# Latent attention's chunk mask: from a bf16 product per score tile to four contraction rows

## What is computed

```python
def attend_mla(q, q_pos, k, v, k_pos):
    s = jnp.einsum('bqhd,bkhd->bhqk', q, k).astype(jnp.float32) * (MLA_QK ** -0.5)
    mask = (k_pos[None, :] // CHUNK) <= (q_pos[:, None] // CHUNK)      # CHUNK = 64
    s = jnp.where(mask[None, None], s, -jnp.inf)
    w = jax.nn.softmax(s, axis=-1).astype(v.dtype)
    return jnp.einsum('bhqk,bkhd->bqhd', w, v)
```

## Time and profile before

| | |
|---|---|
| median of three runs | 1484.28 us |
| span of the profiled execution | 1481.9 us |
| TensorE (PE) busy | 1391.2 us, 94% |
| PE weight load busy | 1121.9 us, 76% |
| VectorE (DVE) busy | 798.2 us, 54% |
| ScalarE (ACT) busy | 637.7 us, 43% |
| latent attention, layer 0 | 206 to 275 us |
| latent attention, layer 1 | 939 to 1008 us |

### The profile page before, as it was taken

One profiled execution on the slowest core, in us unless ns is written; L12 is line 12 of the kernel. 1 busy time (PEld: TensorE's weight loads), 2 busy tenths in 40 slices (PEclk: granted clock), 3 DMA queues, 4 the chain that ended last, 5 costly groups with the idle time before them and its releaser, 6 DMA issues.

```text
span 1481.9 us, 20955 instructions
## 1 busy us (share of the span) xinstructions
PE 1391.2 (94%) x8418; PEld 1121.9 (76%) x8418; DVE 798.2 (54%) x1159; ACT 637.7 (43%) x931; POOL 90.8 (6%) x84
## 2 busy tenths in 40 slices
PE   5998999999999989999889999999999999899996
PEld 5994665799999856777579856558999987567763
DVE  4427534633435347887662383455343444578876
ACT  5327644522324244656343385444222232355651
POOL 0310000000000011100203000000000000110002
PEclk9999998999999989999989999989999999999998
DMA  8233300033225357998812102000233163599965
GB/s 270 72 101 104 114 1 0 1 114 113 64 68 213 158 226 268 412 414 319 269 57 74 60 21 94 1 1 29 86 113 106 39 238 128 216 347 412 415 230 195
DMA packets 95415, 228.45 MB, mean 154 GB/s; under 512 B 14378, under 2 KB 64580, under 8 KB 82372
## 3 DMA queue, kind: packets, MB, share of 16 engines
q1 hardware_dynamic: 83252, 179.58, 33.6%
q0 software_dynamic: 7424, 30.94, 5.9%
q10 hardware_dynamic: 4656, 16.78, 2.8%
HBM read 198.73 MB, written 33.79 MB: 157 GB/s over the span
## 4 chain that ended last, share of the span: by engine, by line
PE 84%; DVE 6%; ACT 5%; DMA 3%; issue 2%; SPq 0%; ACTq 0%; DVEq 0%; POOLq 0%
PE ps L843 10%; PE ps L845 10%; PE ps L844 10%; PE ps L1316 8%; PE ps L1292 4%; PE ps L1294 4%; PE ps L1293 4%; PE ps L1138 3%; PE ps L869 3%; PE ps L872 2%; PE ps L1099 2%; PE ps L875 2%; DMA rows_back<-xrow_d,row_of 2%; PE ps L1279 2%; PE ps L1195 2%; PE ps L1193 2%
## 5 line engine op out<-in xcount | busy, mean ns | idle before, releaser
L1854 DVE TENSOR_TENSOR work<-work,ps 128x544 f32<-128x544 f32 x48 | 34.6, 721 | 208.9 <-ACT work L1673 208.9
L1673 ACT ACTIVATE work<-ps 128x544 f32<-128x544 f32 x48 | 30.0, 626 | 244.9 <-PE ps L845 244.9
L844 PE MATMUL ps<-xn_r,ksv_r 128*128 128x272 f32 x384 | 110.7, 288 | 0.0
L844 PE MATMUL ps<-xn_r,work_r 128*128 128x272 f32 x384 | 110.7, 288 | 0.0
L761 POOL DMA_INDIRECT rows_back<-xrow_d,row_of x32 | 38.2, 1195 | 1120.9 <-DVE row_of L2229 904.4
L1294 PE MATMUL ps<-ew_r,rows_tok_r 128*128 128x512 f32 x256 | 100.0, 391 | 0.0
L1854 DVE TENSOR_TENSOR ew_r<-ew,gu_hi_a_r 128x2048 fp32r<-128x2048 f32 x32 | 73.1, 2290 | 15.4 <-ACT gu_hi_a_r L1696 15.4
L844 PEld LDWEIGHTS ps<-xn_r,ksv_r 128*128 128x128 f32 x384 | 72.2, 188 | 0.0
L844 PEld LDWEIGHTS ps<-xn_r,work_r 128*128 128x128 f32 x384 | 72.2, 188 | 0.0
L1696 ACT ACTIVATE gu_hi_a_r<-ew 128x2048 fp32r<-128x2048 f32 x32 | 60.7, 1908 | 5.6 <-ACT yo_b L1741 5.6
L1316 PE MATMUL ps<-ew,acts 128*128 128x512 f32 x128 | 58.4, 599 | 1.4 <-DVE acts L2346 1.4
(11 more groups left out here) (401 smaller groups left out, 3930.8 us busy)
## 6 DMA issues: line engine op xcount, KB each, us to landing
wr<-in_w_in SPq DMA_DIRECT2D x68, 512.0 KB, 4.7
ew<-in_w_exp_gate SPq DMA_DIRECT2D x32, 1024.0 KB, 7.2
ew<-in_w_exp_up SPq DMA_DIRECT2D x32, 1024.0 KB, 10.9
ew<-in_w_exp_down SPq DMA_DIRECT2D x32, 1024.0 KB
wr<-in_w_out SPq DMA_DIRECT2D x16, 512.0 KB, 4.3
rows_d<-yo_a ACTq DMA_DIRECT2D x14, 512.0 KB
rows_d<-yo_b ACTq DMA_DIRECT2D x14, 512.0 KB
rows_d<-in_zeros POOLq DMA_DIRECT2D x10, 512.0 KB, 9.7
```

What stands on the lines that cost most here:

```text
L844: mm(out_[h], w_hi, x_lo[:, c], start=False, stop=False, skip_group_check=True)
L1854: return v_.tensor_tensor(o_, a, b, op)
```

## The change

The mask becomes part of the product. Keys and queries get four more contraction rows, 96 to 99, one for each query tile x: the keys' row x is -1e30 for the last 64 keys of tile x and zero elsewhere, the queries' row x is 1 for the first 64 queries of tile x and zero elsewhere. The rows are computed on the host (`chunk_rows`) as two new constants, and SyncE loads them in each layer into `kT` and `qT`, 4 partitions of 6400 and of 4352 numbers, before the loop of the gate weights. TensorE waits for both before its first score product. The sample's units keep 96 rows. The semaphore `reload_` becomes `masks_then_x`, which counts 32 for the two loads and 48 after the residual rows. Three of the 12 fills go.

```diff
--- before.py
+++ after.py
@@ -40,6 +40,7 @@
 C_POOL, C_Q, C_KV, C_KR = 0, 256, 512, 640
 C_QS, C_KS, C_VS, C_GATE = 672, 928, 1184, 1440
 HEADS, NOPE, VD, QK = 8, 64, 64, 96
+MR = SEQ // P
 SBH = 4
 HR = ROPE // 2
 NE, NG, EPG, DE = 16, 4, 4, 256
@@ -70,7 +71,7 @@
 K_ID, K_NTRI, K_STRI, K_COS, K_SIN, K_INVC, K_JL, K_VALID, K_STEP, K_TILE, K_E128, K_IOTA, K_TOK = (
     sum(n for _, n in CONST_COLS[:i]) for i in range(len(CONST_COLS)))
 NCONST = sum(n for _, n in CONST_COLS)
-DVE_FILLS = 12
+DVE_FILLS = 9
 TAIL = NE - 2
 JOINT_BANKS = [0, 2, 4, 0, 2]
 END_BANKS = [0, 2, 4, 6, 0]
@@ -115,8 +116,6 @@
         tok_w = sb("tok_w", [P, 2, NTILE, 4], FP16)
         ident_h = sb("ident_h", [P, P], FP16)
         sums_r = sb("sums_r", [P, 2, P], F32R)
-        negrow = sb("negrow", [1, 64], BF16)
-        halfrow = sb("halfrow", [1, P], BF16)
         ident_b = sb("ident_b", [P, P], BF16)
         late_b = sb("late_b", [P, P], BF16)
         rt = sb("rt", [P, 1252 + 80])
@@ -338,7 +337,7 @@
         xn_rdy = sem("xn_rdy", DC + 1)
         ones_in = (xn_rdy[0], DC + 1, DC)
         spill = sem("spill", 16 + 16 * NTILE)
-        reload_ = sem("reload", 16)
+        masks_then_x = sem("masks_then_x", 32 + 16)
         tk_mm = sem("tk_mm", 20)
         tk_ev = sem("tk_ev", 20)
         cm_mm = sem("cm_mm", 4)
@@ -630,6 +629,12 @@
                     sp.dma_start(row(out[nm], l).rearrange("o b t c -> (o b t) c"),
                                  pool_out[1:16, c:c + 256]).then_inc(outs[0], 16)
 
+                sp.wait_ge(tp_mm[0], at(tp_mm, l, 10))
+                sp.wait_ge(xn_rdy[0], at(xn_rdy, l, DC))
+                stand(sp)
+                sp.dma_start(kT[QK:QK + MR, :, :].rearrange("p h n -> p (h n)"), A["late_keys"]).then_inc(masks_then_x[0], 16)
+                sp.dma_start(qT[QK:QK + MR, :, :].rearrange("p h n -> p (h n)"), A["early_queries"]).then_inc(masks_then_x[0], 16)
+
                 with sp.Fori(0, 4) as dp:
                     for b, (nm, k0, k1) in enumerate((("w_br_pool", 0, 2), ("w_br_mla", 2, 6), ("w_br_sb", 6, 8))):
                         if b == 0:
@@ -660,7 +665,7 @@
                 sp.wait_ge(br_mm[0], at(br_mm, l, 24))
                 stand(sp)
                 sp.wait_ge(spill[0], at(spill, l, 16))
-                sp.dma_start(moe["x_keep"][:, :], xres_d).then_inc(reload_[0], 16)
+                sp.dma_start(moe["x_keep"][:, :], xres_d).then_inc(masks_then_x[0], 16)
                 with nc.allow_non_contiguous_dma(reason="one gain row for all partitions"):
                     sp.dma_start(gain_ffn, mat("g_ffn_norm").to_broadcast([P, D])).then_inc(gain_in[0], 16)
                 load_gate_up(l, 0, 0)
@@ -1096,8 +1101,7 @@
                                      start=True, stop=True, skip_group_check=True)
                     else:
                         nk = P * (x + 1)
-                        mm(bank(n % 4, nk), qT[0:QK, h, TO[x]:TO[x] + P], kT[0:QK, h, 0:nk], start=True, stop=False, skip_group_check=True)
-                        ins = mm(bank(n % 4, 64, P, nk - 64), halfrow[:, :], negrow[:, :], start=False, stop=True, skip_group_check=True)
+                        ins = mm(bank(n % 4, nk), qT[0:QK + MR, h, TO[x]:TO[x] + P], kT[0:QK + MR, h, 0:nk], start=True, stop=True, skip_group_check=True)
                     ins.then_inc(s_mm[0], 1)
 
                 def turn(n):
@@ -1151,6 +1155,7 @@
                               k == 0, k == DC - 1)
 
                 pe.wait_ge(ones_in[0], at(ones_in, l, 1))
+                pe.wait_ge(masks_then_x[0], at(masks_then_x, l, 32))
                 for n in range(3):
                     scores(n)
                 for n in range(NU):
@@ -1806,9 +1811,6 @@
 
             fill(ones_b[:, :], 1.0)
             fill(oh_b[:, :], 0.0)
-            fill(negrow[:, :], NEG)
-            fill(halfrow[:, 0:64], 1.0)
-            fill(halfrow[:, 64:128], 0.0)
             fill(small[:, :], 1.0)
             fill(hist[0:1, :], 0.0)
             fill(wpl[:, :, :], 0.0)
@@ -2138,7 +2140,7 @@
                 out_low(0, 7)
                 for k in range(DC):
                     out_low(1, k)
-                dve.wait_ge(reload_[0], at(reload_, l, 16))
+                dve.wait_ge(masks_then_x[0], at(masks_then_x, l, 48))
                 dve.wait_ge(gain_in[0], at(gain_in, l, 32))
                 for t in range(NTILE):
                     m = TM[t]
@@ -2426,6 +2428,15 @@
                 placed(DEPTH - 1, t, END_BANKS)
 
 
+def chunk_rows():
+
+    keys, queries = np.zeros((MR, HEADS, KEYS), np.float32), np.zeros((MR, HEADS, T), np.float32)
+    for x in range(MR):
+        keys[x, :, P * x + P // 2:P * x + P] = NEG
+        queries[x, :, P * x:P * x + P // 2] = 1.0
+    return keys.reshape(MR, -1), queries.reshape(MR, -1)
+
+
 def constants():
 
     con = np.zeros((P, NCONST), np.float32)
@@ -2471,6 +2482,7 @@
     arrays, A, out = {}, {}, {}
     given = {name: np.ascontiguousarray(inputs[name]) for name in _INS}
     given["con"] = constants()
+    given["late_keys"], given["early_queries"] = chunk_rows()
     given["zeros"] = np.zeros((P, D), np.float32)
     for name, a in given.items():
         arrays[f"in_{name}"] = a
```

## The result

The change takes 1465.45 us (median of six runs, 1460.83 to 1469.01), against 1487.78 for the kernel before (six runs, three of them new, 1483.64 to 1496.17). The medians are 22.3 us apart. The ratio is 0.984, with a 95% interval of 0.981 to 0.987, which is some 24 us; 11.8 were forecast. Measured twice more, on two chips, it came to 0.983 (0.980 to 0.987) and 0.984 (0.981 to 0.987).

A forecast was written before the change was run, and what follows sets the result against it. PE was taken to bound the latent attention, with ACT's chain next. Head by head, gains sum to 6.0 us a layer, less 0.1: 11.8 in both, 1470.1 of span, 1472.5 us as median; range 1465 to 1480.5.

The forecast's parts named there:

- The slot of the small product: Layer's masked tiles: each small mask product costs TensorE 0.27 us before transposes, 0.33 before values; at most 18.2 us in both layers.
- ScalarE's order as the next bound: Plain head: ACT's in-order list makes PE wait 0.48 us, so 0.67 of 1.14 is gained; head 5.91, was 6.58.
- the head at clock 0.50 ..., all four, 1.2: Head at half clock, PE busy 11.00 of 11 us: all four small products are gained, 1.2 us a layer.
- opening, up to the first values: Start of a layer's stage: nine small products, 2.6 us raw, less waits of 0.35 and 0.15; gain 2.05.
- first plain head: Ordinary head of the latent attention: 0.67 us gained of 1.14; two plain heads a layer give 1.3.
- the head in which ACT rounds: Head where ACT also rounds an operand: PE already waits 0.36 us, nearly all of its three becomes waiting; gain 0.1.
- the sample's units, the head at 0.50, the plain head behind it: Later stage: around the sample's units 0.4 of 0.8 plus 0.6, half-clock head 1.2, and a plain head's gain.
- the last with three: Last head of a layer with three small products: 0.35 us gained of 0.8.
- The clock: Last three heads of each layer: added PE waits keep the clock down, slower, 1491 us from two such heads; chance 0.05.
- The Trainium skill's 25 ns: Small product: about 60 cycles, making all 64 cost 1.6 us, too little to measure; the prediction set this aside.
- only the slot returns: Rival: longer steps beside the small product stay; 7.5 us gained, 1477, or 2 to 3 and 1482; chance 0.22 in all.
- PE keeps it all: Rival: ACT's chain is less stiff than read, so all 18.2 us are gained, 1466 us; chance 0.08.

The follow-up runs named there:

- The product over 128 rows: Kernel before with its bf16 mask product contracted over 128 rows, 127 of them zero, instead of one: 0.990 of before; on a second chip 0.988, 1470.58 us.
- The reordering: ScalarE's denominator logarithm and exponential each one score exponential later: in the change 1459.43 us (0.978), again 1457.24 us (0.979); in the kernel before 0.997.

## Why the prediction was too small

**What held.** The slot of the small product (0.27 and 0.33 us), that 100 rows are free, that the loads are hidden, ScalarE's order as the next bound, with a plain head of 5.91 forecast and 5.95 found. The reordering then showed that wait for what it was: 7 to 9 us in the change, nothing before.

**What failed** is a term of the sum: "the head at clock 0.50 ..., all four, 1.2". It took the stretch at 0.50 as given and priced four products inside it. The products were what held it open: 13.7 us became 6.8. The first two profiles, taken apart between the starts of the heads' values, show that the miss lies there and not in the other terms (gains in us):

| part of the stage | forecast | layer 0 | layer 1 |
|---|---|---|---|
| opening, up to the first values | 2.05 | 2.00 | 2.00 |
| first plain head | 0.65 | 0.63 | 0.63 |
| the head in which ACT rounds | 0.1 | 0.10 | 0.10 |
| the sample's units, the head at 0.50, the plain head behind it | 2.85 | 5.23 | 5.53 |
| the last with three | 0.35 | 0.14 | 0.14 |

With the sample's 1.0 and the plain head's 0.65 as forecast, the term was 3.6 and 3.9, not 1.2. What the longer stretch costs can be read from the change alone: its stages are 57.7 us with nothing at 0.50, 59.4 with 3.4 and 60.7 to 60.9 with 6.8, so 6.8 us at 0.50 cost some 3 us. In all profiles together: where a product of one row stood behind the sample's products, the stage had 10.2 us or more at 0.50, in 14 of 14 layers; where none did, 6.8 or less, in 22 of 22.

The clock was among the rivals, with the wrong sign and the wrong cause: I looked for it in the waits that would be added. With those added the stretch was shorter, not longer.

**The rest** is in the kernel before, and one profile did not show it. Its three profiles have stages of 138.1, 136.8 and 146.0 us a kernel, the change's three 121.6, 121.5 and 117.1: on average 20.2 apart, of 24.2 in the spans. The other 4.0 lie outside, where all kernels have 42 to 72 us at 0.50 (some 10 of them at the kernel's very end) that differ from run to run: 48.3, 51.9 and 72.0 in the three profiles before, 54.3, 44.0 and 52.3 in the change's. The third profile before makes most of that difference, and no run ties it to the change. The 2 to 3 us that the prediction allows for such falls had no row behind it and was too little: at half clock these differences are up to 12 us of time. The forecast was set against a profile (span 1481.9) that is the fastest of the three.

**The Trainium skill's 25 ns** for a product of up to 64 columns, in "TensorE: Matmul & The Clock Gate", section "Back-to-back issue gap", I set against a slot of 0.13 us and put aside as not borne out here. The product over 128 rows has a slot of 33 ns, near it. By the slot, then, only the product over one row disagrees with the Trainium skill's figure.

**The rival "only the slot returns"** is refuted by the same pair: the step ahead of the product is 0.09 shorter when nothing or something with all rows follows. "PE keeps it all" is refuted by the wait at 223.10. Its time, 1466, is what was measured, and that is luck: the gain that went into waits was made up by the clock.

## What to carry to other kernels

Look twice at a matmul of one contraction row between full ones: try to pad it with zero rows, or to fold it into a neighbour's spare rows. Here it cost 0.27 us where its 64 columns over 128 rows cost 0.06. Numbers of rows between one and 96 were not tried. And where TensorE's clock is down, ask what the matmuls in the stretch look like before you take its length as given. When a small thing comes off the bounding engine's list, read the next engine's order at once: the gain that goes into its waits may come back for one moved line.

## What was not expected of the hardware

- A matmul over one row lengthens the step of the full one ahead by 0.09 us, in bf16 and in float32 alike; one over 128 rows doesn't. Why that is, and why such products kept the clock at 0.50 longer, no run here shows.
- In the rows of the kernel before the same stands between products over 128 and over 32 rows: the sample's values step 0.06 among those over 128 and 0.15 where one over 32 follows. In all but two of the 36 layers profiled, a fall of the clock begins among these products or at most some 1 us behind them. It wasn't tried to pad them, so whether their rows have to do with it is open.

```profile
241.37 0.42 PE L1131 MATMUL ps<-work,x_ybr 128*64 128x32 f32 x4
241.72 0.30 PE L1133 MATMUL ps<-work,vv 32*64 32x32 f32 x2
241.94 0.42 PE L1131 MATMUL ps<-work,x_ybr 128*64 128x32 f32 x4
```

- TensorE busy for 98% of a stretch, with 64 of its 349 (and 345) matmuls over one row, had a granted clock of 0.87 and 0.77. The change's stage, with more waits and without such products, had 0.94 to 1.00. A high busy share did not go with a high clock here.
